# Shifting the operands of the f32r products by 64 bytes, and moving a head's wave columns one head later

## The reference, cut to what matters

```python
p = h @ w_in
i_in, z_f, z_b, q_in, gate_a, u_f, gate_f = split_proj(p)
v = to_heads(i_in); q = silu(to_heads(q_in))
k_f, g_f = forget_gate(to_heads(z_f), lb_f)
k_b, g_b = forget_gate(to_heads(z_b), lb_b)
o_f, s_f = chunk_scan(q, k_f, v, g_f, s0_f)
o_b, s_b = chunk_scan(flip(q), flip(k_b), flip(v), flip(g_b), s0_b)
o = headwise_rms_norm(o_f + flip(o_b))          # times hgrn_norm_w
y_a = o * silu(gate_a)
y_f = fourier_mix(u_f, w_four, b_four) * silu(gate_f)
out = concatenate([y_a, y_f]) @ w_out           # then residual and RMSNorm
```

## The kernel before, in words

| product | count (L61 to L63) | columns | moving, stationary before | after |
|---|---|---|---|---|
| `hidden_h` x `head` | 3552 | 512 | 0, 64 | 64, 0 |
| `hidden_h` x `front` | 288 | 512 | 0, 64 | 64, 0 |
| `front` x `hidden_h` | 3072 | 256 | 64, 0 | 0, 64 |
| `front` and `front_hc`, either way | 576 | 256 | 64, 64 | 0, 0 |
| `tail_cw` x `tail_fold` | 384 | 256 | 64, 64 | 64, 0 |
| `tail_tab` x `tail_p` | 384 | 512 | 64, 64 | 64, 0 |
| `tail_w` x `tail_f` | 768 | 512 | 0, 64 | 64, 0 |
| `tail_w` x `tail_a` | 768 | 512 | 64, 64 | 64, 0 |

## Time and profile before

### The profile page before, as it was taken

One profiled execution on the slowest core, in us unless ns is written; L12 is line 12 of the kernel. 1 busy time (PEld: TensorE's weight loads), 2 busy tenths in 40 slices (PEclk: granted clock), 3 DMA queues, 4 the chain that ended last, 5 costly groups with the idle time before them and its releaser, 6 DMA issues.

```text
span 2398.2 us, 50676 instructions
## 1 busy us (share of the span) xinstructions
PE 2315.6 (97%) x22064; PEld 1947.8 (81%) x22064; DVE 1439.4 (60%) x2999; ACT 503.0 (21%) x785; POOL 44.0 (2%) x64
## 2 busy tenths in 40 slices
PE   7899999999999999999999999999986999999997
PEld 3799999989888888778888887888766888888886
DVE  4821111312777777767777777677888775655554
ACT  3611111110121112111211121111113324221221
POOL 0000000000000000000000000000000001000000
PEclk9999999999999999999999999999998999999999
DMA  8332223222333333232333242423225247433441
GB/s 299 138 93 73 80 91 105 86 92 89 110 94 118 103 97 121 90 121 90 99 112 109 91 126 90 122 89 120 78 90 216 110 189 258 172 144 142 171 163 53
DMA packets 215695, 289.70 MB, mean 121 GB/s; under 512 B 13610, under 2 KB 146866, under 8 KB 211890
## 3 DMA queue, kind: packets, MB, share of 16 engines
q1 hardware_dynamic: 128114, 173.33, 21.8%
q10 hardware_dynamic: 79728, 85.34, 10.2%
q0 software_dynamic: 7632, 27.79, 3.8%
HBM read 193.08 MB, written 93.33 MB: 119 GB/s over the span
## 4 chain that ended last, share of the span: by engine, by line
PE 91%; DVE 5%; issue 1%; DMA 1%; SPq 1%; ACT 1%; ACTq 0%; DVEq 0%
PE all_bank L61 26%; PE all_bank L62 24%; PE all_bank L63 24%; PE all_bank L1149 2%; PE all_bank L1150 2%; PE all_bank L1141 2%; PE all_bank L1095 2%; PE all_bank L1111 2%; PE all_bank L1124 1%; PE all_bank L1134 1%; DVE head_inverse L1275 1%; DVE hidden_h_lo L368 1%; DMA head_query<-piece_query 1%; PE all_bank L726 1%; PE all_bank L743 1%
## 5 line engine op out<-in xcount | busy, mean ns | idle before, releaser
L61 PE MATMUL all_bank<-hidden_h_hi,head_hi 128*128 128x512 f32 x1184 | 494.5, 418 | 0.0
L62 PE MATMUL all_bank<-hidden_h_lo,head_hi 128*128 128x512 f32 x1184 | 471.0, 398 | 0.0
L63 PE MATMUL all_bank<-hidden_h_hi,head_lo 128*128 128x512 f32 x1184 | 470.6, 397 | 0.0
L61 PE MATMUL all_bank<-front_hi,hidden_h_hi 128*128 128x256 f32 x1024 | 289.9, 283 | 6.1 <-DVE hidden_h_lo L368 6.1
L62 PE MATMUL all_bank<-front_lo,hidden_h_hi 128*128 128x256 f32 x1024 | 286.3, 280 | 0.0
L63 PE MATMUL all_bank<-front_hi,hidden_h_lo 128*128 128x256 f32 x1024 | 286.1, 279 | 0.0
L1186 ACT ACTIVATE head_projected<-all_bank 128x512 f32<-128x512 f32 x148 | 88.5, 598 | 890.7 <-PE all_bank L63 890.7
L63 PEld LDWEIGHTS all_bank<-hidden_h_hi,head_lo 128*128 128x128 f32 x1184 | 224.4, 189 | 54.2
L61 PEld LDWEIGHTS all_bank<-hidden_h_hi,head_hi 128*128 128x128 f32 x1184 | 224.5, 190 | 49.6
L62 PEld LDWEIGHTS all_bank<-hidden_h_lo,head_hi 128*128 128x128 f32 x1184 | 224.9, 190 | 43.8
L61 PEld LDWEIGHTS all_bank<-front_hi,hidden_h_hi 128*128 128x128 f32 x1024 | 194.4, 190 | 11.4 <-DVE hidden_h_lo L368 9.3
(11 more groups left out here) (220 smaller groups left out, 4056.8 us busy)
## 6 DMA issues: line engine op xcount, KB each, us to landing
head_raw<-in_w_in POOLq DMA_DIRECT2D x37, 512.0 KB, 5.1
head_value<-value_rows SPq DMA_DIRECT2D x64, 256.0 KB, 5.2
head_query<-piece_query SPq DMA_DIRECT2D x64, 256.0 KB, 6.6
head_out<-head_o ACTq DMA_DIRECT2D x64, 256.0 KB, 5.9
tail_o<-head_out SPq DMA_DIRECT2D x32, 512.0 KB, 5.6
front_raw<-in_w_in SPq DMA_DIRECT2D x17, 512.0 KB, 4.9
front_w_mod<-in_w_ada SPq DMA_DIRECT2D x8, 1024.0 KB, 13.9
front_stage<-in_x SPq DMA_DIRECT2D x16, 512.0 KB, 8.6
```

The lines of the kernel that those rows point to most:

```text
L61: nc.tensor.matmul(out, st_hi, mv_hi, start=start, stop=False)
L62: nc.tensor.matmul(out, st_hi, mv_lo, start=False, stop=False)
L63: return nc.tensor.matmul(out, st_lo, mv_hi, start=False, stop=stop)
```

## The change

Two edits come together.

1. **Places.** A tile `lead` of 64 bytes goes in ahead of the slab, so `base` is byte 17088, at 64. The work area moves to `base + 128 KB + 192`, which is at 0. In the tail, `fold`, `tail_p` and the rows area come to 0, `tail_cw_hi`, `tail_cw_lo` and the tables stay at 64, and some small tiles are packed closer. The table above has the outcome. No instruction is added or removed by this.
2. **Pieces.** The wave columns of head 6 (the seventh head) are projected in head 7's steps and no longer in head 6's. Head 6 has four pieces and head 7 three. Slots 2 and 6 stay empty in both heads (`EIGHT`), and the last step stays empty: 8, 8, 8, 8 halves in head 6 (before 10, 10, 10, 10) and 8, 8, 8, 0 in head 7 (before 6, 5, 5, 0). Counters that were `5 * h`, `10 * h` and `20 * h` are taken from `FIRST_PIECE` and `FIRST_UNIT`, with equal values up to head 6.

```diff
+HALF_LINE = 64
...
-    HALVES = 2 * NG * len(PIECE_SLOT)
-    PER_STEP = HALVES // NG
-    LAST_SLOTS = ((1, 3, 5, 6, 7, 9), (1, 3, 5, 7, 9), (1, 3, 5, 7, 9), ())
+    PIECES_OF = [[(name, h + 1) for name in OF_NEXT] + [(name, h) for name in OF_THIS] for h in range(HEADS - 2)]
+    PIECES_OF += [[(name, HEADS - 1) for name in OF_NEXT] + [("gate_f", HEADS - 2)],
+                  [("wave", HEADS - 2)] + [(name, HEADS - 1) for name in OF_THIS]]
+    EIGHT = (0, 1, 3, 4, 5, 7, 8, 9)
+    SLOTS_OF = [[tuple(range(10))] * NG] * (HEADS - 2) + [[EIGHT] * NG, [EIGHT] * (NG - 1) + [()]]
+    FIRST_PIECE = [sum(map(len, PIECES_OF[:h])) for h in range(HEADS + 1)]
+    FIRST_UNIT = [NG * n for n in FIRST_PIECE]
...
+    def halves_at(h, g, slot):
+
+        return sum(map(len, SLOTS_OF[h][:g])) + SLOTS_OF[h][g].index(slot) if slot in SLOTS_OF[h][g] else None
...
-                        wait_count(sp, proj_stored[b], (10 * h + 6) * DMA)
+                        wait_count(sp, proj_stored[b], (FIRST_UNIT[h] // 2 + 6) * DMA)
...
-        def split_due(g, level, last):
-            for j in range(0, len(pieces(0, last)) - 1):
-                half = 2 * NG * j + 2
-                if last:
-                    step, slot = 0, LAST_SLOTS[0][half]
-                else:
-                    step, slot = half // PER_STEP, half % PER_STEP
+        def split_due(h, g, level):
+            for j in range(len(PIECES_OF[h]) - 1):
+                step, slot = [(i, slot) for i, slots in enumerate(SLOTS_OF[h]) for slot in slots][2 * NG * j + 2]
                 if (step, max(1, min(slot - 2, 4))) == (g, level):
                     return j + 1
...
-    FOLD, SMALL_W, TAB, PARTS, ROWS, LITTLE = 0, 64 * KB + 64, 80 * KB + 64, 144 * KB + 64, 176 * KB + 64, 204 * KB + 64
+    FOLD, SMALL_W, TAB = 0, 64 * KB + HALF_LINE, 80 * KB + 2 * HALF_LINE
+    PARTS, ROWS, LITTLE = (i * KB + 3 * HALF_LINE for i in (144, 176, 204))
...
-    cw_hi, cw_lo = (at(n, [P, 2, CC, FC], SMALL_W + (8 + 4 * i) * KB, F32R) for i, n in enumerate(("cw_hi", "cw_lo")))
+    cw_hi, cw_lo = (at(n, [P, 2, CC, FC], SMALL_W + HALF_LINE + (8 + 4 * i) * KB, F32R) for i, n in enumerate(("cw_hi", "cw_lo")))
...
+        r.sb("lead", [P, HALF_LINE], U8)
         base = r.slab("room", TAIL_ROOM)
         bank = [r.ps(f"bank{i}") for i in range(8)]
-        work = base + 128 * KB + 64
+        work = base + 128 * KB + 3 * HALF_LINE
```

More of the change, by code:

```diff
@@ L972, in _, with turn @@
     def _(pool):
-        def turn(h, last, first=0):
-            for j, (name, head) in list(enumerate(pieces(h, last)))[first:]:
-                wait_count(pool, lo_done, 5 * h + j)
+        def turn(h, first=0):
+            for j, (name, head) in list(enumerate(PIECES_OF[h]))[first:]:
+                wait_count(pool, lo_done, FIRST_PIECE[h] + j)
                 pool.dma_start(raw[:], w_view[:, :, bass.ds(PIECES[name][0] + head * P, P)]).then_inc(w_here, DMA)
         pool.wait_ge(handed.z_done, HEADS)
-        name, head = pieces(0, False)[0]
+        name, head = PIECES_OF[0][0]
         pool.dma_start(raw[:], w_view[:, :, bass.ds(PIECES[name][0] + head * P, P)]).then_inc(w_here, DMA)
@@ L996, in _ @@
                 front_room.clear(pool)
-        turn(HEADS - 1, True)
+        turn(HEADS - 1)
     @block.sync
@@ L1060, in _, with project_half @@
     def _(pe):
-        def project_half(h, last, g, slot):
-            n = halves_at(g, slot, last)
+        def project_half(h, g, slot):
+            n = halves_at(h, g, slot)
             if n is None:
@@ L1173, in freed_units, with evacuate @@
             if j == 0:
-                return 20 * h
-            return 20 * h + NG * (j - 1)
-        def evacuate(h, last, g, slot):
-            n = halves_at(g, slot, last)
+                return FIRST_UNIT[h]
+            return FIRST_UNIT[h] + NG * (j - 1)
+        def evacuate(h, g, slot):
+            n = halves_at(h, g, slot)
             if n is None or n % 2 == 0:
@@ L1182, in evacuate @@
             j, group = unit // NG, unit % NG
-            name, head = pieces(h, last)[j]
-            wait_count(act, proj_done, 20 * h + unit + 1)
-            wait_count(act, proj_stored[unit % 2], (10 * h + unit // 2) * DMA)
+            name, head = PIECES_OF[h][j]
+            wait_count(act, proj_done, FIRST_UNIT[h] + unit + 1)
+            wait_count(act, proj_stored[unit % 2], (FIRST_UNIT[h] // 2 + unit // 2) * DMA)
             nc.scalar.activation(projected[unit % 2][:], ps_proj[unit % 2][:], PIECES[name][1],
                                  scale=PIECES[name][2]).then_inc(proj_copied, 1)
-            wait_count(act, proj_copied, 20 * h + unit + 1)
+            wait_count(act, proj_copied, FIRST_UNIT[h] + unit + 1)
             act.dma_start(scratch[name][bass.ds(head * P, P), group * GRP:(group + 1) * GRP],
                           projected[unit % 2][:]).then_inc(proj_stored[unit % 2], DMA)
-            if group == 0 and j + 1 < len(pieces(h, last)):
+            if group == 0 and j + 1 < len(PIECES_OF[h]):
                 split_high(h, j + 1)
@@ L1196, in step @@
             for slot in range(9):
-                evacuate(h, last, g, slot)
+                evacuate(h, g, slot)
             for d in range(2):
```

64 lines of the change are left out of this document (29 added, 35 removed).

## The result

The changed kernel takes 2387.48 us (median of 10 runs, 2379.38 to 2396.71), the kernel before beside it 2402.07 us. The ratio is 0.9936, 95% interval 0.9926 to 0.9947: faster by 15 us, where 38.4 were forecast. The 2387 lie inside the wide range on record (2338 to 2392, which took in rivals 1 to 3), but outside the forecast's own (2350 to 2378). The profiled execution has a span of 2382.9 us, 15.3 less than before.

A forecast was written before the change was run, and what follows sets the result against it. PE's time was taken as the bound. Heads -27.7, tail -13.9, front -3.0 and +29.6, context 0, pieces -23.4 sum to -38.4 us: 2361.7 from the profiled run, 2365 from the median; own range 2350 to 2378, wide 2338 to 2392.

The forecast's parts named there:

- what bounds the kernel now: Whole kernel: PE's time bounds it; moving at 0 costs 5.9 ns, stationary at 64 2.2 to 6.7 ns, and both add.
- Front rows: Front, `front` moving over `hidden_h`: 3072 products go to (0, 64), the worst pair, 125.9 ns against 115.6: +29.6 us.
- Rival 3: The moving place is free at 256 columns, so front rows pay only the stationary cost: 2348 us; chance 15%.
- Heads 0 to 5: 24 steps of 120 products go from 233.3 to 223.0 ns, -29.7 us; net -27.7 after second steps' +2.
- Tail: `tail_f` -7.9, `tail_a` -3.4, `tail_tab` -1.8, `tail_cw` -0.8 us from the new places, together -13.9.
- The second steps: Heads 0 to 5: in six second steps, part of the gain turns into longer waits on the ACT, DVE, PE chain: +2 us.
- Rival 2: The stationary place is free at 512 columns, whose products go to 227.4 ns: 2387 us; chance 13%.
- Rival 1: The place does nothing, only columns count, and only the pieces bring a gain: 2383 us; chance 8%.
- Pieces: Head 6's first to head 7's third step: seven steps of 33.1 us, 231.7 against 255.15, so -23.4 us.
- lie badly: Pieces' upper bound: 34.5 us a step (-14 us) if the empty slots 2 and 6 lie badly.
- Rival 5: Front rows: the weight load comes out from behind the 256-column product; slower, 2471 us at 160 ns; chance 7%.
- rival 4: DVE takes over in the heads, full steps wait wherever products end earlier: 2396 us; chance 6%.

The follow-up runs named there:

- the map: A separate kernel without the computation, making only unbroken runs of 96 f32r products over a grid of operand places; seven 512-column runs measured 226.6 to 233.4 ns.
- the shifted kernel: The changed kernel with 64 tiny transposes (128 more PE records) added at its very start; measured ratio 0.9923 (0.9907 to 0.9940).

## Why the prediction was half right

The direction held, and the wide range; the size did not. The step that failed is the theory of **what bounds the kernel now**: "both costs hold at either width and add up". The cost of the moving place had been read at 512 columns only, that of the stationary place at 256 only, and all places within 128 bytes; the heads' (64, 0) and the front rows' (0, 64) each needed the one carried over to the other width. What replaced it is one difference within 256 bytes:

- *Front rows*, +29.6 forecast: d goes from 64 to 192, mean 115.6 to 116.6 ns (computed from all start times), 3 us. "The worst pair" does not exist at 256 columns; there d = 0 is the worst of the multiples of 64, and no `front` x `hidden_h` product had it, before or after. Rival 3 (moving free at 256) was nearer here, with +12.5, for another reason. `hidden_h` x `front`, -3.0 forecast, gave 288 x 3.6 = -1.0. The context products stayed at d = 0 and 120 ns, so their 0 was right.
- *Heads 0 to 5*, -27.7: d goes from 192 to 64, 233.3 to 229.7 ns, 2880 x 3.6 = -10.4, and -8.2 was measured. The (64, 0) of 223 that I interpolated is 229.0 in the map.
- *Tail*, -13.9: +3.9 measured. `tail_a` and `tail_tab` went from d = 0 to 192; by the means of all their starts that is 768 x 5.8 + 384 x 4.8 = +6.3. `tail_f` stayed at 192 but for 48 products, and `tail_cw` gained 384 x 2.8 = -1.1. The comparison of `tail_f` with `tail_a` in one loop was sound as a row; that the moving place was its cause was not, since nothing else was varied.
- *The second steps* went from 40.04 to 39.78, 0.1 us less than a full step gained, so they kept waiting for the state chain about as before; the +2 was right in kind, and too large with products that gained little.

The errors of the front and of the heads with the tail have opposite signs (-24.3 against +37.3; the pieces add 10.1), which is why the total was off by 23 us and not by 47. Rival 2 gave 2387, the measured time, and is wrong as well: it has the front rows at +29.6 and the heads at 227.4 ns. A time that fits does not show a mechanism; the intervals do. Rival 1 (the place does nothing) is out by the map, with 6.8 ns between places at 512 columns.

**Pieces**, -23.4 forecast, -13.3 measured: mechanism right, size off. The step of 33.1 us is there (33.07 in head 6's third), with its clock, and no remainder stands between the reciprocals. The term that was mis-sized is "I take 33.1": the seven steps took 34.6 on average, the bound of 34.5 that was named for slots that "lie badly". What this bound stood for was priced at nothing in the middle: the empty slot 2. It leaves one slot between two groups of small products, and blocks of instructions come late there, five pauses and 7.6 us in the seven steps, which are gone in the three kernels with slot 2 full. I had such pauses ahead of me in the earlier trace rows, 5.1 us of "issue" in head 7, 2.7 of them in its first three steps, and explained all of head 7's loss by DVE. The sum also set 7 full steps of eight halves against a stretch that begins behind slot 0 and holds 55 halves, not 56; one half is 2.7 us where PE sets the step, so the miss is rather larger than 10. *Head 7's clock* was 1.00 in two of its three steps. *SP's load* came late once, as allowed for: DVE waits 1.38 us for `head_query` in head 7's first step. Rival 5 did not happen, nor did rival 4: full steps have no idle PE.

What stays open: which of the two levels a run of 256 columns takes; what sets the start of a block's transfer, and so why it is late at some boundaries and not at others; and the one long pause of 3.5 to 5.5 us in the heads, which stands at record 20673 in eight of eleven profiles and at 28609, behind large products, in the shifted kernel, and is missing in two. There the packet starts only 1.0 to 3.1 us after PE has run dry. Counted with the slower clock behind it, it makes a step of head 3 take 45.3 us for 38.6, as much as many an edit is worth.

## What to carry to other kernels

Read a cost of placement from pairs in which one thing differs, and map it with a small kernel before extrapolating: for f32r products of 512 columns let both operands start at the same place within 256 bytes, and expect little of it in runs as short as 12. For 256 columns the best found are differences of 112 and 192 bytes, the latter not always. A pause without a releaser is worth a count of records: if all stand at one number modulo 256, look whether a packet of the instruction queue lands just ahead of its end, and spread large products between the groups of small ones. Moving the program against the blocks moves the pauses; that it pays was not shown. Which slots stay empty matters (2382 to 2399 us for the same work).

## What the runs showed of the hardware

- The interval of f32r products depends on the difference of the operands' starts within 256 bytes: 226.7 to 233.5 ns at 512 columns and 113.3 to 119.9 at 256 for multiples of 64, up to 234.7 and 120.0 for multiples of 16, at clock 1.00 (map of places). The Trainium skill (TensorE: Matmul & The Clock Gate, Back-to-back issue gap) gives the gap of an isolated product by columns alone, 216 ns for 512; no steady run here has a mean under 226.6.
- At 256 columns the order of the multiples of 64 is turned round: d = 0 is the slowest (119.8 to 119.9) and d = 192 mostly the fastest (113.3 to 113.7).
- A run of 512-column products at d = 0 behind small ones takes about six intervals (229 to 236 ns) to reach its steady 227.
- PE can run dry of instructions: between 600 and 1800 us all pauses of 0.9 to 5.5 us without an engine behind them stand at one place within blocks of 256 records, and end 1.2 to 1.6 us after a 16384-byte packet of the instruction queue has landed.
